# Forming the high and low weight halves of both projections by GpSimd transfers, in a two-layer fp32 transformer block

## What is computed

```
h = rms_norm(x, mix_pre_g) * (1 + scale_m) + shift_m
proj = h @ w_in                       # q, k, v, x_lru, gate: 14 column tiles of 128
attn = sliding_window_attention(...)  # 8 heads, window of 128, with sinks
lru = rg_lru(causal_dwconv(x_lru)) * gelu(gate)
x = x + gate_m * rms_norm(concat(rms_norm(attn), rms_norm(lru)) @ w_out)   # 8 tiles
h = rms_norm(x, ffn_pre_g) * (1 + scale_f) + shift_f
x = x + gate_f * rms_norm(conv_ffn(h, w_up, w_down))                       # 72 tiles
```

## Time and profile before

| | |
|---|---|
| runs (us) | 1308.88, 1309.05, 1312.97; median 1309.05 |
| profiled execution, its own time | 1311.93 us |
| its span | 1310.1 us, mean granted clock 0.949 |
| busy: PE, DVE, ACT, POOL | 1195.8, 814.9, 541.1, 109.4 us |
| weight transfers of 512 KB in the ring | 182, all from SP |

### The profile page before, as it was taken

How to read it: one execution, slowest core, us unless ns; L and a number is a source line. 1 busy time by engine, 2 the same in 40 slices (tenths; PEclk the granted TensorE clock), 3 DMA queues, 4 the chain that set the end, 5 groups by cost and what they waited for, 6 DMA issues and landing times.

```text
span 1310.1 us, 13589 instructions
## 1 busy us (share of the span) xinstructions
PE 1195.8 (91%) x5476; PEld 967.6 (74%) x5476; DVE 814.9 (62%) x1094; ACT 541.1 (41%) x712; POOL 109.4 (8%) x108
## 2 busy tenths in 40 slices
PE   5878889699999999999979769989999999999995
PEld 4656668477888888888858558766788888888884
DVE  5786767738777777777463658453764466446644
ACT  4367553434513441344242765343542244224430
POOL 1121330110000000000021023111000000000001
PEclk7989889898999999999989889899999999999997
DMA  9422227314476447642201210120322232222311
GB/s 358 154 84 99 96 95 247 123 49 184 153 265 217 145 145 264 218 145 97 98 32 62 83 49 33 50 80 1 129 97 97 97 97 98 97 97 98 97 61 64
DMA packets 43966, 155.61 MB, mean 119 GB/s; under 512 B 5120, under 2 KB 5376, under 8 KB 43904
## 3 DMA queue, kind: packets, MB, share of 16 engines
q1 hardware_dynamic: 43760, 154.23, 33.9%
q10 hardware_dynamic: 144, 0.52, 0.1%
HBM read 152.64 MB, written 2.10 MB: 118 GB/s over the span
## 4 chain that ended last, share of the span: by engine, by line
PE 74%; DVE 15%; ACT 7%; DMA 2%; POOL 1%; issue 1%; SPq 0%; DVEq 0%; ACTq 0%
PE ps L1142 73%; DMA sb_raw<-in_w 2%; DVE sb_y L1071 1%; DVE sb_wL L789 1%; DVE sb_x L1075 1%; DVE sb_xc L992 1%; ACT sb_scr L658 1%; DVE sb_adaw L795 1%; ACT sb_wH L527 1%; DVE sb_stage L795 1%; POOL sb_I L492 1%; ACT L609 1%; DVE sb_wL L918 1%; PE ps L1308 1%; DVE sb_y L849 0%
## 5 line engine op out<-in xcount | busy, mean ns | idle before, releaser
L1142 PE MATMUL ps<-sb_hH,sb_wH 128*128 128x512 f32 x992 | 400.8, 404 | 19.2 <-DVE sb_wL L918 8.2
L1142 PE MATMUL ps<-sb_hH,sb_wL 128*128 128x512 f32 x992 | 393.4, 397 | 0.0
L1142 PE MATMUL ps<-sb_hL,sb_wH 128*128 128x512 f32 x992 | 371.1, 394 | 1.5 <-POOL sb_hL L458 1.5
L527 ACT ACTIVATE sb_wH<-sb_raw 128x1024 fp32r<-128x1024 f32 x182 | 191.7, 1053 | 165.7 <-DMA sb_raw<-in_w 165.4
L789 DVE TENSOR_TENSOR sb_wL<-sb_raw,sb_wH 128x1024 fp32r<-128x1024 f32 x182 | 222.3, 1221 | 47.9 <-ACT sb_wH L527 47.8
L1142 PEld LDWEIGHTS ps<-sb_hH,sb_wH 128*128 128x128 f32 x992 | 191.6, 193 | 66.9 <-DVE sb_wL L918 8.9
L1142 PEld LDWEIGHTS ps<-sb_hH,sb_wL 128*128 128x128 f32 x992 | 191.4, 193 | 40.7
L1142 PEld LDWEIGHTS ps<-sb_hL,sb_wH 128*128 128x128 f32 x992 | 188.8, 191 | 43.0 <-issue 2.0
L1142 PE MATMUL ps<-sb_mH,sb_wH 128*128 128x512 f32 x512 | 201.4, 393 | 3.2 <-ACT sb_mH L565 3.2
L1142 PE MATMUL ps<-sb_mL,sb_wH 128*128 128x512 f32 x512 | 201.4, 393 | 0.5 <-POOL sb_mL L458 0.4
L1142 PE MATMUL ps<-sb_mH,sb_wL 128*128 128x512 f32 x512 | 201.1, 393 | 0.0
(11 more groups left out here) (192 smaller groups left out, 995.6 us busy)
## 6 DMA issues: line engine op xcount, KB each, us to landing
sb_raw<-in_w SPq DMA_DIRECT2D x182, 512.0 KB, 3.5
sb_adaw<-in_ada SPq DMA_DIRECT2D x44, 512.0 KB, 3.6
sb_vw<-in_ada SPq DMA_DIRECT2D x18, 512.0 KB, 4.7
sb_scr<-in_ada SPq DMA_DIRECT2D x18, 512.0 KB, 5.0
sb_stage<-in_ada SPq DMA_DIRECT2D x16, 512.0 KB, 14.1
sb_raw<-in_w SPq DMA_DIRECT2D x8, 384.0 KB, 14.2
sb_x<-in_x SPq DMA_DIRECT2D x4, 512.0 KB, 6.0
out<-sb_x SPq DMA_DIRECT2D x8, 256.0 KB, 2.1
```

The costliest lines, as they stand in the source:

```text
L527: nc.scalar.activation(chunk_of(wH, n), chunk_of(raw, n), ACT.Copy).then_inc(w_hi, 1)
L1142: return nc.tensor.matmul(out, a, b, start=start, stop=stop, **kw)
```

## The change

For 32 chunks (`by_dma`: 12 to 21 in layer 0, 94 to 115 in layer 1, which is every chunk of both projections from the twelfth of the stream) SP no longer loads `raw` and DVE no longer subtracts. POOL starts a transfer from DRAM (fp32) into `wH` (fp32r), in which the type change rounds. ACT then writes `wL = -wH`. POOL starts a second transfer of the same chunk which adds to what stands in `wL`. PE waits for that one (`w_add`). Both are started by `weights(m)`: the rounding one of chunk m+5, behind a wait for chunk m-1 to be done, then the adding one of chunk m+4, behind a wait for ACT's copy. ACT's `split_step` keeps its place in ACT's program and now waits for `w_cast`.

```diff
--- before.py
+++ after.py
@@ -198,8 +198,21 @@
                 return t[:, kt * SLAB + n * P:kt * SLAB + (n + 1) * P]
             return t[:, slot(n) * KT * P + kt * P:slot(n) * KT * P + (kt + 1) * P]
 
+        def by_dma(n):
+
+            return n >= 2 * GRP and n % NCH < FFN0
+
         def w_no(n):
             return n - GRP + 1
+
+        def lo_no(n):
+            return sum(not by_dma(m) for m in range(GRP, n + 1))
+
+        def add_no(n):
+            return sum(by_dma(m) and slot(m) == slot(n) for m in range(n + 1)) * 16
+
+        def plain_no(n):
+            return sum(not by_dma(m) and m >= GRP and slot(m) == slot(n) for m in range(n + 1)) * 16
 
         def cols_bank(m):
             return bank(1 if m in (norm_no(0, 0), norm_no(1, 0)) else 7)
@@ -222,6 +235,8 @@
         gain1 = tiny[:, 96:104]
 
         w_in = [sem(f"w_in{i}") for i in range(SLOTS_W)]
+        w_cast = [sem(f"w_cast{i}") for i in range(SLOTS_W)]
+        w_add = [sem(f"w_add{i}") for i in range(SLOTS_W)]
         slab_in = [sem(f"slab_in{i}") for i in range(KT)]
         slab_hi, slab_lo, group_kt = sem("slab_hi"), sem("slab_lo"), sem("group_kt")
         w_hi, w_lo = sem("w_hi"), sem("w_lo")
@@ -377,7 +392,7 @@
 
             def refill(n):
 
-                if n >= DEPTH * NCH:
+                if n >= DEPTH * NCH or by_dma(n):
                     return
                 if n < 2 * GRP:
                     sp.wait_ge(*[(group_kt, 2), (group_kt, 3), (group_kt, 4), (group_kt, 6),
@@ -474,6 +489,17 @@
             link(GTS(spl[:, :, :], s3, 8.0, 0.0, ALU.mult, ALU.add))
             GTS(nspl[:, :, :], s3, -16.0, 0.0, ALU.mult, ALU.add).then_inc(sp_ready, 1)
 
+            def weights(m, cast=True):
+
+                n = m + SLOTS_W - 1
+                if cast and n < DEPTH * NCH and by_dma(n):
+                    pool.wait_ge(chunk_done, n - SLOTS_W + 1)
+                    nc.gpsimd.dma_start(chunk_of(wH, n), A["w"][n]).then_inc(w_cast[slot(n)], 16)
+                n = m + SLOTS_W - 2
+                if n < DEPTH * NCH and by_dma(n) and (n % NCH != GRP - 1 or not cast):
+                    pool.wait_ge(w_hi, w_no(n))
+                    nc.gpsimd.dma_start(chunk_of(wL, n), A["w"][n], accum_op=ALU.add).then_inc(w_add[slot(n)], 16)
+
             def add_to_x(l, k):
 
                 for j in X_POOL:
@@ -482,16 +508,22 @@
 
             for l in range(DEPTH):
 
+                B = l * NCH
+                for i in range(1 if l else GRP, GRP):
+                    weights(B + i)
                 for j in range(LT):
+                    weights(B + GRP + j)
                     pool.wait_ge(sig_done, l * LT + j + 1)
                     GTT(I[:, j, :], I[:, j, :], xc[:, j, :], ALU.mult).then_inc(gated_ready, 1)
 
+                weights(B + GRP + LT)
                 pool.wait_ge(root_ready, l + 1)
                 for j in range(LT):
                     pool.wait_ge(gated_ready, l * LT + j + 1)
                     GTT(I[:, j, :], I[:, j, :], R[:, j, :], ALU.mult).then_inc(drive_ready, 1)
 
                 for t in range(QT - 1):
+                    weights(B + GRP + LT + 1 + t)
                     pool.wait_ge(den_ready, l * (QT - 1) + t + 1)
                     sc = scores[t % 2].rearrange("p (s k) -> p s k", s=NQ)
                     GTT(sc, sc, den[t % 2].unsqueeze(2).broadcast_to([P, NQ, P]), ALU.mult).then_inc(p_ready, 1)
@@ -504,10 +536,16 @@
                         pool.wait_ge(*proj_release(l, NPROJ - 1))
                     GTT(yt(AT + j), yt(AT + j), xc[:, j, :], ALU.mult).then_inc(l_ready, 1)
                 lo_tiles(conv_no(l, 0), mL, mH, False, yt)
+                for j in range(NOUT):
+                    weights(B + NPROJ + j)
                 add_to_x(l, 0)
                 lo_tiles(conv_no(l, 1), hL, hH, True, yt)
+                for i in range(GRP):
+                    weights(B + NCH - GRP + i)
                 add_to_x(l, 1)
                 if l + 1 < DEPTH:
+                    weights(B + NCH)
+                    weights(B + NCH + 1, False)
                     lo_tiles(conv_no(l, 2), hL, hH, True, yt)
         NCONST = 9
 
@@ -523,7 +561,12 @@
 
                 if n >= DEPTH * NCH:
                     return
-                act.wait_ge(w_in[slot(n)], n // SLOTS_W * 16)
+                if by_dma(n):
+                    act.wait_ge(w_cast[slot(n)], add_no(n))
+                    nc.scalar.activation(chunk_of(wL, n), chunk_of(wH, n).bitcast(fp32), ACT.Copy,
+                                         scale=-1.0).then_inc(w_hi, 1)
+                    return
+                act.wait_ge(w_in[slot(n)], plain_no(n))
                 nc.scalar.activation(chunk_of(wH, n), chunk_of(raw, n), ACT.Copy).then_inc(w_hi, 1)
 
             def fetch_sqrt():
@@ -1141,9 +1184,16 @@
             def mm(out, a, b, start, stop, **kw):
                 return nc.tensor.matmul(out, a, b, start=start, stop=stop, **kw)
 
+            def weights_ready(n):
+
+                if by_dma(n):
+                    pe.wait_ge(w_add[slot(n)], add_no(n))
+                else:
+                    pe.wait_ge(w_lo, lo_no(n))
+
             def tile_products(acc, n, hi_, lo_, ready=None):
 
-                pe.wait_ge(w_lo, w_no(n))
+                weights_ready(n)
                 for kt in range(KT):
                     a, al = block_of(wH, n, kt), block_of(wL, n, kt)
                     if ready:
@@ -1169,7 +1219,7 @@
                     pe.wait_ge(hi_ready, k0 + kt + 1)
                     for c, b in enumerate(banks):
                         if kt == 0 and not slabs:
-                            pe.wait_ge(w_lo, w_no(n0 + c))
+                            weights_ready(n0 + c)
                         mm(bank(b), block_of(wH, n0 + c, kt), hH[:, kt, :], kt == 0, False)
                         mm(bank(b), block_of(wL, n0 + c, kt), hH[:, kt, :], False, False)
                     if between:
```

## The result

| | before | after |
|---|---|---|
| runs (us) | 1308.88, 1309.05, 1311.82, 1312.97; median 1310.43 | 1341.14, 1344.70, 1347.37, 1347.89; median 1346.03 |
| ratio | | 1.0259, 95% interval 1.0236 to 1.0281 |
| profiled execution, its span, clock | 1311.93, 1310.1, 0.949 | 1347.37, 1345.6, 0.932 |

The change makes the kernel 2.6% slower: 35.6 us by the medians, 35.5 by the spans. The forecast was 21.5 us slower, a median of 1330.5, with a range of 1317 to 1350.

A forecast was written before the change was run, and what follows sets the result against it. PE was taken to bound the feed-forward parts, mostly ACT and POOL the mixers. 13.0 + 0.9 + 2 x 4.2 + 2 x 2.0 - 4.8 = +21.5 us on 1309.05 gave 1330.5, range 1317 to 1350.

The forecast's parts named there:

- part 5: Layer 0's mixer and output projection: DVE splits and raw refills leave the chain, a gain of 4.8 us; layer 1 nothing.
- Part 1: Between the layers: chunk 99's rounding transfer, issued behind the last add to x, delays the root by 13.0 us.
- Part 2: Start of layer 1: DVE loses three splits on its chain, yet starts the k product 0.9 us later, behind ACT.
- Nothing for the adding transfers: Both layers: adding transfers cost 0, each being issued four chunks, 21.8 us, before PE needs it, except chunk 100.
- Part 3: Middle of both mixers: ACT waits for rounding transfers issued behind LRU products, delaying its sigmoids; +4.2 us in each layer.
- Part 4: Before the first score tile: POOL issues two transfers on the path while PE waits; +2.0 us a layer.
- "nothing" for 16.8 MB more traffic: Chunks on the new route: the extra bytes cost 0, since DVE and ACT steps set the pace.
- A (quick transfers): POOL's transfers: issue 0.33 us, landing 3.5 us, so only +12 us, 1321; chance 0.22.
- B (issues stretched by DVE): Ten POOL issues on the path each pay 0.87 us beside DVE: +8.7 us, 1339; chance 0.13.
- C (slow adding transfers that TensorE waits for): Both output projections: adding transfers outlast a chunk's 5.44 us and PE waits, 31 us on top, 1362; chance 0.08.
- D (not slower): Whole kernel: splits and a refill leaving the chain, 16.0 us, offset least costs of 16.2: +0.2, 1309; chance 0.05.

## Why the prediction was right, and where it fell short

The direction and the main mechanism were right: POOL's order puts landings bare on the chain, and the order alone, mended, gives 32.0 of the 35.6 us back. The size was short by 14 us; the measured 1346.0 lies inside the range, near its upper end, and part 5 had the wrong sign.

- **Part 1, boundary: right.** Forecast 13.0, 14.0 in the trace, and 14.8 by the run that undoes it (13.5 by the ratios). The eight sums, sixteen matmuls, took 9.97 in one stretch, as worked out from 8.0 and 1.9 of a lower clock, and the granted clock was at 0.50 when they began.
- **Part 2, start of layer 1: undersized.** 0.9 became some 3.3. I let chunk 102's rounding transfer land after 4.2 us; it took 7.55 (at 738.10), issued 0.6 us behind the first adding one. "Nothing for the adding transfers" was the wrong step. That they slow what lands beside them is shown over the whole kernel (4.5 to 3.9 us with the adding gone); at this one place no run takes the adding away and leaves the order.
- **Part 3, loops: right in kind, sized a little low.** 4.2 each became 4.9 in layer 0 (5.25 less the 0.4 that it was late already) and 5.5 in layer 1, with landings of 4.2 to 4.9 for my 4.2. Moving the transfers a step earlier took these waits away.
- **Part 4, first score tile: right.** 2.0 a layer forecast, 1.5 measured twice, since the issues take 0.55 and 0.91 and not 1.0.
- **Part 5, gains of 4.8: this step failed.** The splits of chunks 17 and 18 left the chain, but only 0.5 us with them, and the out-projection lost time, 1.9 us by the table and some 3.7 over all traces, where I had 2.3 of gain. I counted DVE's work taken off that stage, but not what the adding transfers take from the stage's refills: DMA engines at 0.71 for 0.60 in the window 185 to 245. With the adding made plain the stage takes 56.7 us, as on the old route. Undone alone, the new route of these eight chunks gave 9.8 us back, of which the third landing in the loop and the pair before the score tile belong to parts 3 and 4.
- **"Nothing" for the adding transfers was wrong, "nothing" for 16.8 MB more traffic was not refuted.** Made plain, the same transfers with the same bytes cost some 6.5 us less, and that kernel is no slower than the one before (0.9969).
- **The end, for which I had nothing.** 2.4 us lie behind the last update of x. This end takes 2.64 us before, 3.36 to 3.72 in the kernels with 22 to 24 chunks on the new route, and 4.96 to 5.05 in the six with 32, plain or adding. So it goes with the number of transfers from POOL; what runs there no row shows, and the cause stays open.
- **Left over:** -2.0 in layer 0's feed-forward part and the other +2.5 of the last row. Each is within what the runs of one kernel differ by (6.8 us). The mean clock was 0.932 for 0.949, and this was not traced further.

Rivals. A (quick transfers) falls: issues of 0.33 and landings of 3.5 were not seen. B (issues stretched by DVE) falls as a price: the longest issue took 0.94 us. The Trainium skill's rule named beside it ("SBUF — State Buffer", section "SBUF: two separate sides") speaks of descriptors that are written late, which could also show in the landings, 10.9 us at most here; no run isolates it. C (slow adding transfers that TensorE waits for) falls in its own form: TensorE waited for one transfer, 4.2 us, and not sixteen times. Its half that adding is slow holds: 6.8 us, near the 7 at which I had set its point. D (not slower) did not come, and its reason, 16 us leaving the chain, is not seen. Near its 1309 lies the mended order, 1314.1 us (1.0018), and with layer 0's out-projection on the old route 1308.6 (0.9978).

## What to carry to other kernels

When transfers move to the queue of an engine that also computes, price first their place in that engine's order: a landing of 4 to 5 us costs nothing if it is issued one step earlier, and all of itself if issued behind the product that its consumer waits for. Count a saved instruction only where its engine ends the stage's last wait (36 us off DVE were worth 2 to 3 us at one place), and charge a transfer that adds to its destination, even one that lands in time, to the refills that run beside it.

## What was not expected of the hardware

- An adding transfer of 512 KB takes longer than a rounding one from the same queue: 6.8 us for 4.5 (median of 32 each), and it takes more of the DMA engines for the same bytes, 11.5% for 8.4% of the span over both kinds. If the whole difference is the adding half's, that half costs 7.3 where a plain one costs 4.2, an estimate of 1.7 times as much.
- It also stretches others: rounding transfers beside it took 4.5 us, and 3.9 with the adding gone.
- Its issue holds POOL longer as well, 0.89 us for 0.59.
- The span goes on longer behind the last update of x the more transfers POOL has started: 2.64 us with none of these chunks, 3.36 with 22 and 5.0 with 32.
